# Expert layers: weight slots filled ahead in the preceding projection, and the first two blocks' rows made by one-hot products in the routing

## The chip, the cores and the metric

The kernel runs on one core of a Trainium2 chip. The metric is device time in microseconds of one execution, the median of three runs for the kernel before. Engines are named as in the profile: PE is TensorE (PEld its weight loads), DVE VectorE, ACT ScalarE, POOL GpSimd, SP the queue that issues most DMAs.

## The reference, cut to what matters

A hybrid layer (recurrent unit, sparse attention, gated linear attention, feed-forward) is followed by a second block of two layers: an SSD mixer and a dilated attention mixer, each ending in an output projection with residual and layer norm, and each followed by a mixture of experts. The sequence has 512 tokens of width 1024, all in float32. The change touches only what lies around the two expert layers:

```python
def _hierarchical_moe(x, w_rg, b_rg, w_re, b_re, w_gate, w_up, w_down):
    g_w, g_idx = lax.top_k(jax.nn.softmax(g_logits, axis=-1), 1)      # 1 of 4 groups
    e_w, e_idx = lax.top_k(jax.nn.softmax(e_logits, axis=-1), 2)      # 2 of its 8 experts
    ...
    def expert_block(args):
        xb, e = args
        h = jax.nn.silu(xb @ w_gate[e]) * (xb @ w_up[e])
        return h @ w_down[e]
```

There are 32 experts; w_gate and w_up are 1024 x 512, w_down is 512 x 1024, each 2 MB in float32. Every token goes through two experts, and their outputs are summed with the gate weights.

## The kernel before, in words

`second_block` (L3221) calls for each of the two layers a mixer (`ssd` L2202, `attention` L3043) and then `moe` (L2466). Each mixer ends in `project_model` (L484), the output projection: SP loads the weight row tiles (L505), DVE splits each into a high and a low part (L523, L525), PE multiplies (L538, L548), and the layer norm tail (`LayerNormTail`, L739) normalises token tile by token tile; its SP part (L752) loads the norm's rows and the router's weights. All products of the projection are counted on the semaphore `done`.

A kernel is a chain of stages (L62). In a stage every engine runs its own instruction list; at its end all engines meet at a barrier, and POOL clears the semaphores of an earlier stage. A DMA that is in flight is not waited for by the barrier, only by whoever waits for its semaphore.

`moe` runs two stages. In the first, `moe_route` (L2489), SP stores x to DRAM as x_rows (L2525), for the gathers, and issues nine weight loads: gate, up and down of experts 0 and 1 into slots 0 and 1 (L2529), and, after the router product, of expert 2 into the third slot (L2532), which is made of two buffers that are free there. PE computes the router logits (L2563) and turns them (L2568). DVE chooses the two experts of each token as one-hot rows `oh` (L2617 to L2635). PE ranks each token within its expert and counts the tokens of each expert (L2576, L2579; DVE waits for `counted` at L2643). DVE computes the block and the row of each token (L2646 to L2673), PE makes the lists of rows by one-hot products (L2584, after `placed`), DVE writes them as indices (L2686 to L2688). A block holds up to 64 rows of one expert; blocks 0 to 31 are the experts' first blocks, later ones the overflow. `keep_running(n)` (L2691) issues n products of the identity, whose result nobody reads: 26 and 28 in the routing and 30 at the start of the next stage.

In the second, `moe_experts` (L2704), the blocks alternate between two sets of buffers s. Per block b:

- POOL copies the block's indices to `ex_col` (L2775) and gathers its rows from x_rows (L2778). The gather of block b + 2 waits till the rows of block b are turned (L2795), and POOL issues it after the scatter of block b - 1 and before the scatter of block b.
- PE turns the rows (`turn_x`, L2812), ACT copies them to `xT` (L2877).
- PE multiplies by gate and up, one on each half of the columns of the array (`gate_up`, L2821); ACT makes silu (L2881), DVE multiplies (L2920).
- PE turns the result (`turn_h`, L2829), ACT copies it (L2885), PE multiplies by down (L2838), ACT copies the result (L2890), and POOL scatters it to y_rows (L2785, L2700).

The order on PE is written out for the first blocks (L2842 to L2859) and then looped: gate/up of block b, down of block b - 1, turn_x of block b + 1, turn_h of block b. The weights' order is SP's (L2740 to L2753): gate and up of block b go out when gate/up of the slot's last user is finished (`gate_up_ready`), down when that user's down is finished:

```python
def load(b, e, slot, users):
    for which, used in ((GATE, gate_up_ready), (UP, gate_up_ready), (DOWN, down_ready)):
        sp.wait_ge(used, users)
        sp.dma_start(raw[slot][which], ...).then_inc(w_loaded[slot][which], 16)
load(3, 3, 0, 1)
load(4, 4, 1, 2)
load(5, 5, 0, 4)
```

From block 3 on only slots 0 and 1 are used. At the end SP loads the rows of y_rows back (L2761), and DVE adds them to x with a layer norm.

## Time and profile before

| | |
|---|---|
| median of three runs | 3425.83 us (3418.22 to 3431.83) |
| the profiled execution | 3431.23 us, its span 3429.3 us |
| mean granted clock of PE | 0.923 |
| busy: PE, DVE, ACT, POOL | 3036.2, 1153.5, 852.2, 472.7 us |
| HBM read, written | 596.61 MB, 24.16 MB |
| expert weight loads | 64 of each of gate, up and down, 2048 KB each |

The profile gives the busy time of each engine; times are microseconds from the span's start, and the duration of a group in order of time is its length from first start to last end. A product in float32 makes two MATMUL records, so "x32" are 16 products. PEclk is the granted clock as a share of 2.4 GHz: 1.00 is that level, 0.50 is 1.2 GHz. A DMA share of 1.0 means that the core's 16 DMA engines were busy throughout. In brackets stands how long the engine was idle before an instruction and what released it. The expert layer after the SSD mixer is called layer 0 here (its routing begins at about 1899), the one after attention layer 1 (at about 2831).

### The profile page before, as it was taken

The numbers are of one execution on the slowest core, as the hardware profiler recorded it, in microseconds if no ns is written. First come the engines' busy times: TensorE is split into PE (matmuls) and PEld (weight loads), VectorE is DVE, ScalarE is ACT, GpSimd is POOL, SyncE is SP. The second block draws the span as 40 slices with busy tenths as digits, with TensorE's granted clock in tenths as the row PEclk, the third lists the DMA queues.
The fourth block names the chain that finished last, engine by engine and source line by source line (L and its number), as shares of the span: only waits on it lengthen the run. The fifth ranks groups of instructions, "written<-read, shape, count | busy, mean of one in ns | idle before, by whom it ended". The sixth has DMA issues, their size and how long they took to land. (4 is left out here: it accounts for less than half of the span.)

```text
span 3429.3 us, 41635 instructions
## 1 busy us (share of the span) xinstructions
PE 3036.2 (89%) x16071; PEld 2153.8 (63%) x16071; DVE 1153.5 (34%) x1825; ACT 852.2 (25%) x1731; POOL 472.7 (14%) x670
## 2 busy tenths in 40 slices
PE   7998989899989999999899887888599888888875
PEld 6787769777868878789678533333278765333332
DVE  3553754333353333437364300000253462000002
ACT  2514741332233310114450111111111341111111
POOL 0132510000000000000260111111122321111110
PEclk9998999999989999999689899988799998998897
DMA  3242022133333322222002799999733108999996
GB/s 125 86 103 75 2 74 87 39 86 86 91 93 98 98 85 92 89 84 62 2 30 83 311 362 402 406 397 400 281 114 102 36 21 349 367 394 392 403 399 254
DMA packets 250616, 605.24 MB, mean 176 GB/s; under 512 B 39829, under 2 KB 204051, under 8 KB 225788
## 3 DMA queue, kind: packets, MB, share of 16 engines
q1 hardware_dynamic: 238268, 583.05, 46.9%
q0 software_dynamic: 10880, 16.83, 1.4%
q10 hardware_dynamic: 1344, 3.67, 0.5%
q8 instruction: 82, 1.34, 0.2%
q14 instruction: 42, 0.34, 0.0%
HBM read 596.61 MB, written 24.16 MB: 181 GB/s over the span
## 5 line engine op out<-in xcount | busy, mean ns | idle before, releaser
L2821 PE MATMUL bank<-moe_raw,ex_xT 128*64 128x512 f32 x1984 | 532.7, 698 | 147.2 <-DMA moe_raw<-in_moe_w_up 144.2
L2821 PEld LDWEIGHTS bank<-moe_raw,ex_xT 128*64 128x64 f32 x1984 | 181.2, 159 | 452.4 <-issue 448.0
L2920 DVE TENSOR_TENSOR ex_h<-ex_gate,bank 64x512 f32<-64x512 f32 x64 | 44.1, 690 | 986.9 <-ACT ex_gate L2881 986.9
L248 PE MATMUL bank<-hT_hi,cut_lo 128*128 128x512 f32 x1248 | 313.0, 393 | 0.0
L248 PE MATMUL bank<-hT_hi,ahead 128*128 128x512 f32 x624 | 257.1, 412 | 28.2 <-DVEq L421 16.7
L248 PEld LDWEIGHTS bank<-hT_hi,cut_lo 128*128 128x128 f32 x1248 | 234.5, 188 | 53.3
L248 PE MATMUL bank<-hT_lo,ahead 128*128 128x512 f32 x624 | 254.8, 408 | 0.0
L248 PE MATMUL bank<-hT_hi,cut_hi 128*128 128x512 f32 x624 | 245.0, 393 | 1.2 <-DVE cut_hi L277 1.2
L248 PE MATMUL bank<-hT_lo,cut_hi 128*128 128x512 f32 x624 | 244.6, 392 | 0.0
L2838 PE MATMUL bank<-moe_raw,ex_hT 128*64 128x512 f32 x992 | 224.6, 592 | 1.3 <-ACT ex_hT L2885 1.3
L2881 ACT ACTIVATE ex_gate<-bank 64x512 f32<-64x512 f32 x64 | 37.8, 591 | 666.4 <-PE bank L2821 666.4
L2838 PEld LDWEIGHTS bank<-moe_raw,ex_hT 128*64 128x64 f32 x992 | 80.8, 137 | 132.3 <-issue 132.3
L248 PEld LDWEIGHTS bank<-hT_hi,ahead 128*128 128x128 f32 x624 | 122.8, 197 | 62.7 <-ACTq L1942 11.4
L248 PEld LDWEIGHTS bank<-hT_lo,ahead 128*128 128x128 f32 x624 | 122.7, 197 | 29.8 <-issue 0.2
L277 DVE CAST cut_hi<-raw 128x2048 fp32r<-128x2048 f32 (+1 forms) x66 | 63.8, 966 | 223.1 <-PE bank L248 136.4
L248 PEld LDWEIGHTS bank<-hT_hi,cut_hi 128*128 128x128 f32 x624 | 117.2, 188 | 28.2 <-DVE cut_hi L277 2.1
L248 PEld LDWEIGHTS bank<-hT_lo,cut_hi 128*128 128x128 f32 x624 | 117.2, 188 | 26.3 <-issue 0.2
L279 DVE TENSOR_TENSOR cut_lo<-raw,cut_hi 128x2048 fp32r<-128x2048 f32 (+1 forms) x66 | 120.4, 1824 | 2.3
L100 POOL CAST ahead<-raw 128x2048 fp32r<-128x2048 f32 x5 | 10.6, 2112 | 778.1 <-DMA raw<-in_ssd_w_in 385.0
L2785 POOL COPY moe_to<-moe_place 128x1 uint32 x64 | 11.6, 181 | 767.5 <-ACT moe_y L2890 767.5
L248 PE MATMUL bank<-cut_lo,hT_hi 128*128 128x256 f32 x768 | 108.1, 283 | 0.9 <-DVE cut_lo L279 0.3
L2812 PEld LDWEIGHTS bank<-ident,moe_x 64*128 64x128 f32 x528 | 63.2, 200 | 70.7 <-issue 70.7
(568 smaller groups left out, 5415.1 us busy)
## 6 DMA issues: line engine op xcount, KB each, us to landing
moe_raw<-in_moe_w_gate SPq DMA_DIRECT2D x62, 2048.0 KB, 14.0
moe_raw<-in_moe_w_up SPq DMA_DIRECT2D x62, 2048.0 KB, 18.5
moe_raw<-in_moe_w_down SPq DMA_DIRECT2D x62, 2048.0 KB, 9.6
raw<-in_w_in SPq DMA_DIRECT2D x26, 1024.0 KB, 5.4
raw<-in_w_ffn_in SPq DMA_DIRECT2D x44, 512.0 KB, 5.0
raw<-in_ssd_w_in SPq DMA_DIRECT2D x20, 1024.0 KB, 5.2
raw<-in_attn_w_qkv SPq DMA_DIRECT2D x18, 1024.0 KB, 5.1
raw<-in_w_in SPq DMA_DIRECT2D x24, 512.0 KB, 4.3
```

The costliest lines, as they stand in the source:

```text
L100: self.nc.gpsimd.tensor_copy(self.K.ahead[:, 0:self.words], self.K.raw[:, 0:self.words])
L248: last = nc.tensor.matmul(out, a(pa, k), b(pb, k), start=(late == "hi" and k == 0 and n == 0), stop=(late == "lo" and k == kt - 1 and n == ...
L277: nc.vector.tensor_copy(hi, raw).then_inc(rounded, 1)
L279: return nc.vector.tensor_tensor(lo, raw, hi.bitcast(F32), ALU.subtract)
L2785: nc.gpsimd.tensor_copy(to[:, s:s + 1], place[:, ds(b, 1)]).then_inc(directed, 1)
L2812: last = nc.tensor.transpose(TX[:, k * ER:(k + 1) * ER], x[:, s, k:D:KD], K.ident[0:ER, 0:ER])
L2821: last = nc.tensor.matmul(GU[s][rows, :], xT[:, s, k * ER:(k + 1) * ER], raw[slot][which][:, k * HID:(k + 1) * HID], start=(k == 0), stop= ...
L2838: last = nc.tensor.matmul(DB[s][rows, :], hT[:, s, k * ER:(k + 1) * ER], raw[slot][DOWN][:, k * D + half * HID:k * D + (half + 1) * HID], ...
L2881: nc.scalar.activation(gate[:, s, :], GU[s][left, :], ACT.Silu).then_inc(gate_done, 1)
L2920: nc.vector.tensor_tensor(h[:, s, :], gate[:, s, :], GU[s][right, :], ALU.mult).then_inc(h_ready, 1)
```

## The change

The two expert slots get fixed places in SBUF, known before the mixer runs (`ExpertSlots`), so that they can be filled while the mixer's output projection is still running. Slot 0 is loaded after the projection's own loads, gate and up of slot 1 when the projection's products are all done. In the routing, down of slot 1 and the third slot follow. In the routing the rows of blocks 0 and 1 are no longer gathered: DVE compares each token's rank among experts 0 and 1 with 0 to 63, which gives one-hot columns, and PE multiplies x, which lies in SBUF by token, by them; the result is `xT` for both blocks, already turned. Gate/up of block 0 is also made in the routing, and behind it gate and up of block 3 are loaded into slot 0. The stage of the experts starts with gate/up of block 1, and its gathers with block 2. The 28 and 30 filler products are gone. In the attention layer the projection's split weights lie at another place (`cut_at`).

```diff
@@ project_model @@
+                if slots:
+                    slots.load(sp, 0, 0, (GATE, UP, DOWN))
+                    sp.wait_ge(done, 2 * TT)
+                    slots.load(sp, 1, 1, (GATE, UP))
                 if then and begin:
@@ new @@
+FIRST = 2
+class ExpertSlots:
+    WORDS = 6 * WN
+    def __init__(self, nc, K, A, layer):
+        self.base = nc.sbuf_base
+        matrix = lambda n: self.base + 4 * n * WN
+        self.places = ((matrix(0), matrix(1), matrix(4)), (matrix(2), matrix(3), matrix(5)))
...
+    def load(self, sp, slot, e, matrices):
+        for which in matrices:
+            sp.dma_start(self.raw[slot][which], self.weights[which][e]).then_inc(self.loaded[slot][which], 16)
@@ moe_route, sync @@
-                for e in range(2):
-                    for which in range(3):
-                        sp.dma_start(raw[e][which], weights_d[which][e]).then_inc(K.w_loaded[e][which], 16)
+                K.slots.load(sp, 1, 1, (DOWN,))
                 sp.wait_ge(product_ready, 1)
-                for which in range(3):
-                    sp.dma_start(raw[2][which], weights_d[which][2]).then_inc(K.w_loaded[2][which], 16)
+                K.slots.load(sp, 2, 2, (GATE, UP, DOWN))
+                sp.wait_ge(first_gate_up, 1)
+                K.slots.load(sp, 0, 3, (GATE, UP))
@@ moe_route, tensor @@
                 last.then_inc(counted, 1)
-                keep_running(nc, K, 28)
+                pe.wait_ge(dealt, 1)
+                for k in range(KD):
+                    for t in range(TT):
+                        last = nc.tensor.matmul(first_bank[:, k], K.x[:, t, k:D:KD], first_oh[:, t], start=(t == 0), stop=(t == TT - 1))
+                last.then_inc(first_turned, 1)
                 pe.wait_ge(placed, 1)
...
                 last.then_inc(listed, 1)
+                pe.wait_ge(first_kept, 1)
+                pe.wait_ge(K.w_loaded[0][GATE], 16)
+                pe.wait_ge(K.w_loaded[0][UP], 16)
+                for k in range(KD):
+                    for which, rows in ((GATE, slice(0, ER)), (UP, slice(ER, 2 * ER))):
+                        last = nc.tensor.matmul(K.bank[0][rows, :], xT[:, 0, k * ER:(k + 1) * ER], raw[0][which][:, k * HID:(k + 1) * HID],
+                                                start=(k == 0), stop=(k == KD - 1))
+                last.then_inc(first_gate_up, 1)
@@ moe_route, scalar @@
+                act.wait_ge(first_turned, 1)
+                for e in range(FIRST):
+                    nc.scalar.activation(xT[:, e, :].rearrange("p (k r) -> p k r", k=KD), first_bank[:, :, e * ER:(e + 1) * ER], ACT.Copy).then_inc(first_kept, 1)
@@ moe_route, vector @@
+                done(nc.vector.tensor_scalar(first_rank[:, :, :], oh[:, 2, :, 0:FIRST], -2.0 * S, 2.0 * S, ALU.mult, ALU.add))
                 dve.wait_ge(counted, 1)
                 ranks = K.bank[1][:, 0:TT * NE].rearrange("p (t e) -> p t e", t=TT)
+                done(nc.vector.tensor_tensor(first_rank[:, :, :], first_rank[:, :, :], ranks[:, :, 0:FIRST], ALU.add))
+                nc.vector.tensor_tensor(first_oh[:, :, :, :], ..., ALU.is_equal).then_inc(dealt, 1)
@@ moe_experts, sync @@
-                load(3, 3, 0, 1)
+                load(3, 3, 0, 1, (DOWN,))
@@ moe_experts, gpsimd @@
-                gather(0, 0)
-                gather(1, 1)
+                for s in range(2):
+                    gather(s, FIRST + s)
+                for s in range(2):
+                    scatter(s, s)
                 n = pairs_used(pool)
-                with pool.Fori(0, n) as i:
+                with pool.Fori(1, n) as i:
@@ moe_experts, tensor @@
                 pe.sem_inc(y_kept, 2)
-                keep_running(nc, K, 30)
-                turn_x(0, 0)
-                gate_up(0, 0, 0, 16)
-                turn_x(1, 0)
+                pe.sem_inc(gate_up_ready, 1)
+                pe.sem_inc(x_turned, FIRST)
+                pe.sem_inc(x_kept, FIRST)
+                gate_up(1, 0, 1, 16)
                 turn_h(0, 0)
-                gate_up(1, 0, 1, 16)
                 down(0, 0, 0, 16)
@@ moe_experts, scalar @@
-                keep_x(0, 0)
                 make_gate(0, 0)
-                keep_x(1, 1)
@@ attention @@
-        project_model(nc, K, A.attn_w_o_2[0], HW // P, oT, tail(mem), cut_at=qk_at)
+        project_model(nc, K, A.attn_w_o_2[0], HW // P, oT, tail(mem), cut_at=K.slots.places[1][GATE], slots=K.slots)
```

## Rows read from the trace of the kernel before

**Rows 1.** DMA busy by slice of the span, from the page (40 slices of 85.7 us).

```profile
DMA  3242022133333322222002799999733108999996
```

**Rows 2.** chain of waits inside layer 1's expert loop: start, us, what.

```profile
2957.02 22.34 DMA moe_raw<-in_moe_w_up
2979.49 7.09 PE bank L2821 x32
2986.58 3.45 PE bank L2838 x16
```

**Rows 3.** busy time by stretch, layer 0: us, engines, clock, DMA share, GB/s.

```profile
1880.00:1890.00 10.00, 8.35 (x45) 6.79 (x43) 9.55 (x17) 4.92 (x10) 0.00 (x0) 1.00 0.00 0
1920.00:1930.00 10.00, 10.00 (x65) 10.00 (x64) 8.43 (x25) 0.00 (x0) 0.00 (x0) 0.69 0.99 421
2000.00:2010.00 10.00, 10.00 (x54) 4.57 (x50) 0.69 (x1) 1.40 (x3) 1.15 (x2) 1.00 0.66 240
```

**Rows 4.** SP's DMA issues around layer 0: start, us, line, transfer.

```profile
1857.01 1.29 SPq L729 DMA_DIRECT2D router_whole<-in_moe_w_router_expert  x1
1900.26 0.51 SPq L2529 DMA_DIRECT2D moe_raw<-in_moe_w_gate  x1
1909.07 0.45 SPq L2532 DMA_DIRECT2D raw<-in_moe_w_down  x1
1955.30 0.33 SPq L2744 DMA_DIRECT2D moe_raw<-in_moe_w_gate  x1
2008.76 0.33 SPq L2744 DMA_DIRECT2D moe_raw<-in_moe_w_down  x1
```

**Rows 5.** TensorE in order of time, layer 0: start, us, work, idle before.

```profile
1909.38 6.07 PE L2695 MATMUL bank<-ident 128*128 128x128 f32 x52
1919.10 1.60 PE L2579 MATMUL bank<-rt_oh,rt_ones 128*128 128x32 f32 x8
1920.52 9.23 PE L2695 MATMUL bank<-ident 128*128 128x128 f32 x56
1929.58 1.88 PE L2584 MATMUL bank<-rt_block_oh,rt_row_oh 128*128 128x48 f32 x16
1944.72 1.07 PE L2812 MATMUL bank<-ident,moe_x 64*128 64x64 f32 x8 [3.10 <-DMA moe_x<-x_rows,ex_col]
1946.48 8.78 PE L2821 MATMUL bank<-moe_raw,ex_xT 128*64 128x512 f32 x32 [0.69 <-ACT ex_xT L2877]
1957.36 7.09 PE L2821 MATMUL bank<-moe_raw,ex_xT 128*64 128x512 f32 x32
1964.28 3.60 PE L2838 MATMUL bank<-moe_raw,ex_hT 128*64 128x512 f32 x16
1982.34 1.06 PE L2812 MATMUL bank<-ident,moe_x 64*128 64x64 f32 x8 [2.23 <-DMA moe_x<-x_rows,ex_col]
```

**Rows 6.** other engines in order of time, layer 0.

```profile
1920.81 0.19 DVE L2646 COPY rt_cnt<-bank 128x32 f32<-128x32 f32 x1 [3.03 <-PE bank L2579]
1926.02 1.23 DVE L2665 TENSOR_TENSOR rt_row_oh<-rt_iota_r,rt_row 128x1024 f32<-128x1024 f32 x1
1932.91 2.29 DVE L2915 TENSOR_SCALAR x_tok<-x_tok 128x4096 f32<-128x4096 f32 x1 [0.54 <-PEq L69]
1933.74 1.50 POOL L2775 COPY ex_col<-moe_idx 64x1 uint32<-64x1 uint32 x1 [26.28 <-issue]
1945.83 0.60 ACT L2877 ACTIVATE ex_xT<-bank 128x512 f32<-128x512 f32 x1 [28.86 <-PE bank L2812]
```

**Rows 7.** layer 1 in order of time: SP's issue, then TensorE.

```profile
2889.54 0.34 SPq L2744 DMA_DIRECT2D moe_raw<-in_moe_w_gate  x1
2851.21 1.85 PE L2579 MATMUL bank<-rt_oh,rt_ones 128*128 128x32 f32 x8
2879.50 10.00 PE L2821 MATMUL bank<-moe_raw,ex_xT 128*64 128x512 f32 x32 [0.69 <-ACT ex_xT L2877]
2916.73 1.07 PE L2812 MATMUL bank<-ident,moe_x 64*128 64x64 f32 x8 [2.38 <-DMA moe_x<-x_rows,ex_col]
```

More of the change, by code:

```diff
@@ L481, with project_model @@
     on_pool = None
[L484 removed]
+def project_model(nc, K, w, kt, x, tail, fresh=None, begin=True, row_scale=None, cut_at=None, slots=None):
     SLOTS = 3
@@ L2463, in expert_weights @@
             A.moe_w_down_2[layer].rearrange("e (p k) m -> e p (k m)", p=P))
+class ExpertSlots:
[4 more added lines that the diff above has]
+        self.places = ((matrix(0), matrix(1), matrix(4)), (matrix(2), matrix(3), matrix(5)))
+        self.raw = [[nc.alloc_sbuf_tensor_at(f"slot{layer}_{s}_{which}", [P, WN], F32, offset=place) for which, place in enumerate(places)]
+                    for s, places in enumerate(self.places)]
+        self.raw.append([K.third[:, :WN], K.third[:, WN:], K.raw[:, :]])
+        self.raw = [[x[:, :] for x in slot] for slot in self.raw]
+        self.loaded = [[nc.alloc_semaphore(f"w_loaded{layer}_{s}_{which}") for which in range(3)] for s in range(3)]
+        self.weights = expert_weights(A, layer)
+    def load(self, sp, slot, e, matrices):
+        for which in matrices:
+            sp.dma_start(self.raw[slot][which], self.weights[which][e]).then_inc(self.loaded[slot][which], 16)
 def moe(nc, K, A, layer, tail):
@@ L2473, in moe @@
         idx, place = sb("idx", [ER, NB + 2], U32), sb("place", [P, NB], U32)
-        K.w_loaded = [[nc.alloc_semaphore(f"w_loaded{layer}_{s}_{which}") for which in range(3)] for s in range(3)]
         x, y, to = sb("x", [ER, 2, D]), sb("y", [P, 2, HID]), sb("to", [P, 2], U32)
+        xT = sb("xT", [P, 2, KD * ER])
         K.y_stored = [nc.alloc_semaphore(f"y_stored{layer}_{s}") for s in range(2)]
@@ L2479, in moe, with moe_route @@
         K.picked = [nc.alloc_semaphore(f"picked{layer}_{n}") for n in range(2 * TT)]
-        raw_at = -(-nc.sbuf_base // 32) * 32
-        with nc.sbuf_tensor(f"moe{layer}_raw", [P, 2, 3, WN], F32) as raw:
-            picked = nc.alloc_sbuf_tensor_at(f"picked{layer}", [P, 2, TT, D], F32, offset=raw_at)
-            K.tail_junk = nc.alloc_sbuf_tensor_at(f"tail_junk{layer}", [P, D], F32, offset=raw_at + 4 * 2 * TT * D)
-            raw = [[raw[:, s, which, :] for which in range(3)] for s in range(2)] + [[K.third[:, :WN], K.third[:, WN:], K.raw[:, :]]]
-            moe_route(nc, K, A, layer, weight, expert, pairs, idx, place, raw, x, y, to)
-            moe_experts(nc, K, A, layer, expert, pairs, idx, place, raw, x, y, to, weight, picked, tail)
-def moe_route(nc, K, A, layer, weight, expert, pairs, idx, place, raw, x, y, to):
+        picked = nc.alloc_sbuf_tensor_at(f"picked{layer}", [P, 2, TT, D], F32, offset=at)
+        K.tail_junk = nc.alloc_sbuf_tensor_at(f"tail_junk{layer}", [P, D], F32, offset=at + 4 * 2 * TT * D)
+        K.w_loaded = K.slots.loaded
+        moe_route(nc, K, A, layer, weight, expert, pairs, idx, place, K.slots.raw, x, y, to, xT)
+        moe_experts(nc, K, A, layer, expert, pairs, idx, place, K.slots.raw, x, y, to, xT, weight, picked, tail)
+def moe_route(nc, K, A, layer, weight, expert, pairs, idx, place, raw, x, y, to, xT):
     K.x_rows = nc.dram_tensor(f"x_rows{layer}", (S, D), F32, kind="Internal").ap()
-    weights_d = expert_weights(A, layer)
     with ExitStack() as mem:
@@ L2701, in store_rows, with moe_experts @@
                                  in_=y[:, s, :], in_offset=None, bounds_check=4 * S - 1, oob_is_err=False).then_inc(K.y_stored[s], 16)
-def moe_experts(nc, K, A, layer, expert, pairs, idx, place, raw, x, y, to, weight, picked, tail):
+def moe_experts(nc, K, A, layer, expert, pairs, idx, place, raw, x, y, to, xT, weight, picked, tail):
     weights_d = expert_weights(A, layer)
@@ L2739, in _, with load @@
             def _(sp):
-                def load(b, e, slot, users):
-                    for which, used in ((GATE, gate_up_ready), (UP, gate_up_ready), (DOWN, down_ready)):
+                def load(b, e, slot, users, matrices=(GATE, UP, DOWN)):
+                    for which in matrices:
+                        used = down_ready if which == DOWN else gate_up_ready
                         sp.wait_ge(used, users)
                         sp.dma_start(raw[slot][which], weights_d[which][ds(e, 1)].rearrange("e p f -> p (e f)")).then_inc(w_loaded[slot][which], 16)
-                load(3, 3, 0, 1)
+                load(3, 3, 0, 1, (DOWN,))
                 load(4, 4, 1, 2)
@@ L3225, in second_block @@
     for layer, mixer in enumerate((ssd, attention)):
-        K.router, K.tail_junk = Router(nc, K, A, layer), None
+        K.router, K.tail_junk, K.slots = Router(nc, K, A, layer), None, ExpertSlots(nc, K, A, layer)
         mixer(nc, K, A, norm(layer, 0, K.hT))
```

21 lines of the change are left out of this document (13 added, 8 removed).

## The prediction

> **What bounds the kernel now.** I began with the page's row of DMA busy time [rows 1]: of 40 slices, two runs stand at 9, and these are the two expert layers. Each streams 32 experts of three 2 MB matrices (6.3 MB), and nothing else in the kernel loads DMA so heavily. The chain of waits in such a stretch [rows 2] alternates a long DMA piece of 18 to 22 us with 7.1 us of gate/up and 3.5 us of down. The DMA piece covers the landing of one load; TensorE needs about 13 us for a block, and the chain takes some 33.6 us for two blocks. In the long middle of a layer the transfer stream is therefore the clock. An earlier start of that stream moves the end of the layer by the same amount, and a faster engine there moves nothing.
>
> Next I asked where the stream is not running. The stretches by 10 us [rows 3] show three things in layer 0: nothing moves at 1880 to 1890 while the preceding projection ends, 421 GB/s at a share of 0.99 during the routing, and a share of only 0.66 at 2000 to 2010. SP's issues [rows 4] say why. The nine loads of blocks 0 to 2 leave from 1900.26 to 1909.5 and last till about 1954. The next goes out at 1955.30, when the gate/up product of block 0 has freed slot 0. The last hole ends with the issue at 2008.76; from there DMA stays at a share near 1.0 to the layer's end. Up to that hole the order is set by TensorE [rows 5]: products to count the ranks, 28 filler products, the list at 1929.58, a barrier, 30 fillers, a wait for gathered rows till 1944.72, their transposes, the copy by ScalarE [rows 6], then gate/up of block 0 from 1946.48 to 1955.26. So the question is how much earlier gate/up of block 0 ends, and what of that is kept till the last hole.
>
> **The change part by part.**
>
> *Loads moved into the projection.* Slot 0 (6.3 MB) is issued after the router loads, at about 1858.5 [rows 4]; gate and up of slot 1 (4.2 MB) when all products of the projection are done. At 421 GB/s [rows 3] that is 15 and 10 us, and DMA is idle or nearly so there. It takes 10.5 MB or 25 us per layer out of the routing. This alone gives nothing: the stream would only stop sooner, at about 1927, and wait for slot 0. It is what permits gate/up of block 0 inside the routing. The issues cost SP about 0.4 to 1.3 us each [rows 4], with nothing urgent behind them. 25 us per layer, 50 in all, is the ceiling.
>
> *One-hot rows in the routing.* Counts are ready at 1920.7 and VectorE takes them at 1920.81 [rows 5, 6]. The small multiply-add before that wait lies in its 3 us of idle time. After it come one small addition (0.2 us, as the copy in rows 6) and a comparison of 512 elements per partition, half of the 1024 that take 1.23 us [rows 6], 0.6 us. So TensorE starts at about 1921.7. The 32 products have the shape of the fillers: 26 of those took 6.07 us, 0.233 each, with the clock at full [rows 5]; 32 are 7.5 us at the 2.4 GHz level and 15 at 1.2 GHz. In the trace the granted clock averages 0.69 over 1920 to 1930 [rows 3], so it stood at the lower level for some 6 us, and 28 fillers took 9.23 us [rows 5]. With 4.4 us of that dip left, 9 products run at half clock and 23 at full: 9.7 us, to 1931.4. Bounds 7.5 and 15; I take 9.7 because the dip is in both layers at this place.
>
> *Its operand is strided.* The stationary operand x_tok is read at every eighth float. The nearest row is the transposes of gathered rows, strided alike: eight loads in 1.07 us, 0.134 each [rows 5], against 0.117 for a contiguous filler. So the 64 loads would take 8.6 instead of 7.5 us at most; I charge nothing and keep 1.1 us for the range. The Trainium skill (SBUF — State Buffer, Door 1: The DMA port swizzle) says instead that reads which leave a 16-byte line with each element pay a penalty. By that rule these loads would be slower than contiguous ones; the row hardly shows it, but with 64 partitions, not 128. It is the slow rival below.
>
> *The list and the extra copy.* The list products wait for VectorE, now 0.9 us later (about 1929.4), and for TensorE, 1931.4; they take 1.9 us [rows 5], to 1933.3. The two copies of xT (0.60 us each, rows 6) lie beside them.
>
> *Gate/up of block 0 in the routing.* It begins at 1933.4. A gate/up takes 7.09 us at full clock [rows 5]; 8.78 and 10.0 where a dip fell into it [rows 5, 7]. I take 8.0, so it ends at 1941.4. What vanishes from before it: barrier, fillers, gather, transposes, copy (1931.5 to 1946.5). The next load goes out at 1941.5 instead of 1955.3: **13.8 us earlier**. In layer 1 the counts end at 2853.06 [rows 7]; plus 1.0, 9.7, 1.9, 8.0 and 0.1 makes 2873.8 against 2889.54: **15.7 us earlier**. It gains more because gate/up took 10.0 us there.
>
> *The barrier now lies behind gate/up.* SP issues two loads behind it (0.9 us) and TensorE resumes some 0.55 us after the last engine [rows 6]. From the end of gate/up(0) to the end of down(0) were 12.6 us [rows 5]. Now: 1.5 + 7.1 (gate/up 1) + 0.65 + 0.5 (turn and copy h) + 3.5 = 13.3 to 13.7, so **1.1 us lost** per layer. If SP or the clearing of semaphores drags, up to 3.
>
> *Gathers.* Those of blocks 2 and 3 are issued first after the barrier, at about 1943.5. From copying the index to the first transpose took 11.0 us (1933.74 to 1944.72, rows 5, 6), so block 2's rows are there at about 1955, when down(0) ends: no wait, bounds 0 and 3. Block 3's used to be queued on GpSimd behind the scatter of block 0, and TensorE waited 2.23 and 2.38 us [rows 5, 7]. That wait goes. Late next is block 4, still queued behind the scatter of block 1: 3 us of GpSimd work and 9.5 to 11 of landing against 12.8 us of TensorE work, up to 1.2 us of waiting. I keep **1.7 us gained** per layer, bounds 0 and 4.
>
> *The removed fillers* (28 and 30) never delayed a load. Their cover is the clock; see the first rival. The longer semaphore list and three VectorE instructions in the layer cost under 0.3 us.
>
> *Sum:* 13.8 − 1.1 + 1.7 = 14.4 and 15.7 − 1.1 + 1.7 = 16.3, together 30.7 us. The profiled execution took 3431.23 us (span 3429.3), so the same execution would take 3400.5. It stands 5.4 above the median 3425.83, from which the forecast is 3395.
>
> **The rivals.**
>
> *Clock lost with the fillers.* TensorE now idles about 1 us before the one-hot products where fillers ran. In the rows a dip to half follows stretches with gaps although fillers ran [rows 3, 5]. If all 32 products run at 1.2 GHz (15 us) and gate/up takes 10.0, each layer loses 5.3 + 2.0, in all 14.6, and the gain is 16: 3410. The Trainium skill (TensorE: Matmul & The Clock Gate, Part 1) states that idleness takes the array's clock to half and sustained work gives it back; by it this case could come in either layer. For it: three new short waits. Against: the routing is denser in real work than it was. Chance 0.15, about two thirds of it still beyond 0.5%.
>
> *No dip at all.* Products 7.5 and gate/up 7.1: 3.1 us more per layer, 3389. Against it: dips in both layers [rows 3, 7]. Chance 0.10.
>
> *The one-hot products are slow.* If strided 128-row loads cost 0.58 us each, 64 take 37 us instead of 9.7; each layer loses 27.3 against a gain of 14.4 to 16.3, in all +24: 3450. It decides from about 0.39 us per load, where 25 us eat the gain. Nearest row 0.134 [rows 5]: chance 0.06.
>
> *The early loads give nothing*, since the issue after the routing is not what sets the end, or the slots are not filled ahead. Then about 3426. Against it: the share of 0.66 just before 2010 [rows 3], holes that only TensorE's progress explains. Chance 0.05.
>
> **How the numbers follow.** Forecast 0.64. About 0.5% (17 us) is what a measurement can tell from no change. Faster: 0.64 + 0.10 + 0.10 = 0.84; same: 0.05 + 0.05 = 0.10; slower 0.06. The range goes from the dip-free case less the spread of runs (3418 to 3432) and the upper bound of the gather term, 3378, to the clock case with 3 us for the barrier, 3413.
>
> **What would show it.** Slot 0's loads near 1858 and slot 1's near 1887; x_tok products ending by 1932; the first load into a freed slot near 1941 and 2874; DMA idle some 14 us between 1927 and 1941; steady two-block periods of 33.6 us unchanged; the last hole ending 14 us earlier. Wrong: products of x_tok over 15 us, a gather wait over 3 us at block 2, or a layer whose stream starts earlier but ends at the same distance from its start.

## The result and the profile after

The changed kernel takes 3407.31 us in the median of 20 runs (3396.29 to 3418.59), the kernel before 3429.86 us in 20 runs on the same chips (3417.73 to 3443.50). The ratio is 0.9938, 95% interval 0.9925 to 0.9951: 22.5 us less, where I had forecast 30.7 less (3395 us). The profiled execution took 3402.02 us with a span of 3400.0; its mean granted clock is 0.925 (before 0.923).

DMA busy by slice of the span, after, to be held against [rows 1]. Ahead of the first run of nines 2 and 7 have become 4 and 6, ahead of the second 0 and 8 have become 2 and 6: bytes have moved to earlier slices.

```profile
DMA  3242022134333322222004699999833126999996
```

Busy time by stretch of layer 0, after (columns as in [rows 3]):

```profile
1880.00:1890.00 10.00, 9.12 (x48) 7.42 (x46) 9.56 (x20) 4.40 (x9) 0.00 (x0) 1.00 0.18 44
1890.00:1900.00 10.00, 3.14 (x17) 2.54 (x18) 8.73 (x12) 3.58 (x6) 0.00 (x0) 0.64 0.88 375
1920.00:1930.00 10.00, 8.95 (x40) 8.82 (x40) 7.65 (x24) 0.00 (x0) 0.00 (x0) 0.66 0.74 316
1930.00:1940.00 10.00, 10.00 (x52) 9.85 (x54) 2.40 (x10) 1.08 (x2) 0.00 (x0) 1.00 0.01 2
1940.00:1950.00 10.00, 7.82 (x38) 2.56 (x36) 2.47 (x4) 1.88 (x2) 0.78 (x1) 1.00 0.25 74
2000.00:2010.00 10.00, 9.84 (x46) 4.03 (x48) 0.69 (x1) 0.79 (x2) 2.21 (x3) 1.00 0.97 386
```

The same two stretches in the kernel before:

```profile
1930.00:1940.00 10.00, 8.41 (x61) 8.32 (x61) 3.75 (x9) 0.00 (x0) 3.67 (x4) 0.83 1.00 424
1940.00:1950.00 10.00, 6.21 (x33) 3.56 (x33) 0.00 (x0) 1.88 (x2) 1.14 (x2) 0.84 1.01 372
```

The early loads run: 375 GB/s at 1890 to 1900. Then the stream has nothing left to fetch, from about 1927 to 1947: shares 0.01 and 0.25 where it was 1.00 and 1.01 before. That is 20 us of idle DMA where I had reckoned with 14. At 2000 to 2010 the share is 0.97 instead of 0.66, so the last hole has moved forward. SP's issues say by how much (after, layer 0; to be held against [rows 4]):

```profile
1859.08 3.01 SPq L2491 DMA_DIRECT2D slot<-in_moe_w_gate  x1
1887.40 0.33 SPq L2491 DMA_DIRECT2D slot<-in_moe_w_gate  x1
1900.56 0.42 SPq L2554 DMA_DIRECT2D x_rows<-x_tok  x1
1946.83 0.33 SPq L2491 DMA_DIRECT2D slot<-in_moe_w_gate  x1
1960.85 0.33 SPq L2792 DMA_DIRECT2D slot<-in_moe_w_down  x1
1998.29 0.33 SPq L2792 DMA_DIRECT2D slot<-in_moe_w_down  x1
```

Gate of block 3 leaves at 1946.83 (before 1955.30), down of block 3 at 1960.85, and down of block 5, which ends the last hole, at 1998.29 (before 2008.76). The routing starts 0.76 us later in this execution, so from here on I count from the issue of the x_rows store (1900.56 after, 1899.80 before). What TensorE does in that time, after, layer 0 (to be held against [rows 5]):

```profile
1922.57 15.48 PE L2613 MATMUL bank<-rt_first_oh,x_tok 128*128 128x128 f32 x64 [1.05 <-DVE rt_first_oh L2691]
1937.89 1.88 PE L2617 MATMUL bank<-rt_block_oh,rt_row_oh 128*128 128x48 f32 x16
1939.70 7.09 PE L2625 MATMUL bank<-slot,moe_xT 128*64 128x512 f32 x32
1948.97 7.09 PE L2871 MATMUL bank<-slot,moe_xT 128*64 128x512 f32 x32 [2.18 <-PEq L2895]
1957.15 3.65 PE L2888 MATMUL bank<-slot,ex_hT 128*64 128x512 f32 x16 [0.47 <-ACT ex_hT L2934]
1960.98 1.06 PE L2862 MATMUL bank<-ident,moe_x 64*128 64x64 f32 x8 [0.18 <-DMA moe_x<-x_rows,ex_col]
```

and in layer 1 ([rows 7] before):

```profile
2841.23 15.48 PE L2613 MATMUL bank<-rt_first_oh,x_tok 128*128 128x128 f32 x64 [1.05 <-DVE rt_first_oh L2691]
2858.36 7.09 PE L2625 MATMUL bank<-slot,moe_xT 128*64 128x512 f32 x32
2867.97 8.78 PE L2871 MATMUL bank<-slot,moe_xT 128*64 128x512 f32 x32 [2.52 <-PEq L2895]
```

The one-hot products take 15.48 us, in both layers, against my 9.7. The list is as I wrote, gate/up of block 0 is 0.9 us shorter, the barrier behind it cost 1.4 and 3.4 us against my 1.1, and the wait for block 2's rows is 0.18 us. The middle of the layer is as it was: the chain has pieces of DMA of some 18 to 22 us, and between them 7.1 to 10 us of gate/up and 3.5 us of down on TensorE, as before ([rows 2] shows one such round).

### The profile page after: what moved, and what is told of

Its sections match the earlier page's. It is cut to its first block and busy times, and to the rows that moved or that the text cites. A ratio compares the mean times of both kernels' runs of the same rounds, so it can differ in the third digit from the quotient of the medians.

```text
span 3400.0 us, 41341 instructions
## 1 busy us (share of the span) xinstructions
PE 3023.7 (89%) x15935; PEld 2146.2 (63%) x15935; DVE 1154.3 (34%) x1831; ACT 852.0 (25%) x1731; POOL 469.5 (14%) x662
## 5 line engine op out<-in xcount | busy, mean ns | idle before, releaser
L2871 PE MATMUL bank<-slot,moe_xT 128*64 128x512 f32 x1920 | 512.2, 694 | 146.6 <-DMA slot<-in_moe_w_up 139.9
L2871 PEld LDWEIGHTS bank<-slot,moe_xT 128*64 128x64 f32 x1920 | 176.6, 159 | 439.2 <-issue 432.1
L2888 PE MATMUL bank<-slot,ex_hT 128*64 128x512 f32 x992 | 224.8, 592 | 2.3 <-ACT ex_hT L2934 2.3
L2888 PEld LDWEIGHTS bank<-slot,ex_hT 128*64 128x64 f32 x992 | 80.8, 137 | 132.3 <-issue 131.0
L248 PEld LDWEIGHTS bank<-hT_hi,ahead 128*128 128x128 f32 x624 | 123.7, 198 | 62.3 <-ACTq L1946 11.4
L277 DVE CAST cut_hi<-raw 128x2048 fp32r<-128x2048 f32 (+1 forms) x66 | 63.8, 967 | 222.8 <-PE bank L248 136.1
L100 POOL CAST ahead<-raw 128x2048 fp32r<-128x2048 f32 x5 | 10.5, 2092 | 777.6 <-DMA raw<-in_ssd_w_in 385.2
L2833 POOL COPY moe_to<-moe_place 128x1 uint32 (+1 forms) x64 | 11.7, 183 | 730.3 <-ACT moe_y L2939 730.3
L248 PE MATMUL bank<-ahead,hT_hi 128*128 128x256 f32 x384 | 95.6, 284 | 6.3 <-DVEq L421 6.3
```

The source lines that it names most:

```text
L100: self.nc.gpsimd.tensor_copy(self.K.ahead[:, 0:self.words], self.K.raw[:, 0:self.words])
L248: last = nc.tensor.matmul(out, a(pa, k), b(pb, k), start=(late == "hi" and k == 0 and n == 0), stop=(late == "lo" and k == kt - 1 and n == ...
L277: nc.vector.tensor_copy(hi, raw).then_inc(rounded, 1)
L2833: nc.gpsimd.tensor_copy(to[:, s:s + 1], place[:, ds(b, 1)]).then_inc(directed, 1)
L2871: last = nc.tensor.matmul(GU[s][rows, :], xT[:, s, k * ER:(k + 1) * ER], raw[slot][which][:, k * HID:(k + 1) * HID], start=(k == 0), stop= ...
L2888: last = nc.tensor.matmul(DB[s][rows, :], hT[:, s, k * ER:(k + 1) * ER], raw[slot][DOWN][:, k * D + half * HID:k * D + (half + 1) * HID], ...
```

## The experiments

All are compared with the kernel before on the same chips. Since single executions of one kernel lie up to 23 us from its median, I read two things of each: the median, and the distance of the last hole's end (the issue of block 5's down load) from the x_rows store in its profiled execution. A hole is a stretch in which the stream of weight loads stands still. "Holes" is the sum over both layers less the 220.0 us of before; "time" is the difference of the medians.

| kernel | block 3's down (layers 0, 1) | block 5's down | holes | time | ratio, 95% interval |
|---|---|---|---|---|---|
| before | 68.1, 70.0 | 109.0, 111.0 | 0 | 0 | 1 |
| the change | 60.3, 62.3 | 97.7, 99.3 | -22.9 | -22.5 | 0.9938 [0.9925, 0.9951] |
| the change again | 60.2, 62.2 | 98.1, 99.5 | -22.4 | -20.7 | 0.9938 [0.9921, 0.9956] |
| early loads alone | 63.3, 63.0 | 104.9, 105.0 | -10.1 | -7.4 | 0.9976 [0.9957, 0.9994] |
| the same, no 30 fillers | 63.3, 63.8 | 104.1, 105.4 | -10.5 | -6.6 | 0.9975 [0.9964, 0.9987] |
| one-hot rows alone | 60.2, 62.1 | 100.5, 99.2 | -20.3 | -14.6 | 0.9957 [0.9939, 0.9975] |
| contiguous slices of x | 55.9, 56.0 | 93.2, 95.2 | -31.6 | | a single execution, 3400.6 us |
| x copied ahead | 55.9, 56.1 | 93.5, 93.0 | -33.4 | -29.0 | 0.9915 [0.9887, 0.9943] |
| x copied ahead, again | 55.9, 56.1 | 93.4, 93.1 | -33.4 | -28.3 | 0.9910 [0.9896, 0.9925] |
| and earlier gathers | 54.3, 54.9 | 94.0, 91.8 | -34.2 | -38.0 | 0.9888 [0.9867, 0.9908] |
| and earlier gathers, again | 54.0, 54.0 | 93.9, 93.2 | -32.8 | -30.2 | 0.9896 [0.9873, 0.9919] |
| gate/up of block 0 late | 62.2, 62.7 | 99.6, 101.9 | -18.5 | -17.5 | 0.9951 [0.9935, 0.9967] |
| products made twice | 77.1, 77.3 | 116.3, 114.2 | +10.5 | +13.3 | 1.0030 [1.0009, 1.0050] |

The last hole puts kernels whose holes differ by more than 2 us in the order of their times (closer neighbours change places, as -20.3 and -18.5 do), and misses the time by 6 us at most. The end of the last hole is a good place to read this change, also where my numbers for it were not. What differs between the kernels ahead of the store does not explain them: from the load of the router's expert weights to the x_rows store are 42.8 us in layer 0 and 35.0 to 35.1 in layer 1, in the kernel before, in the changed one and in those with either half alone, so the early loads do not lengthen the projection.

### The early loads alone

The kernel before with `ExpertSlots` and the loads of slot 0 and of gate and up of slot 1 in the projection; rows gathered, fillers kept, gate/up of block 0 in the experts' stage.

```diff
@@ kernel before: project_model and moe_route, sync @@
+                if slots:
+                    slots.load(sp, 0, 0, (GATE, UP, DOWN))
+                    sp.wait_ge(done, 2 * TT)
+                    slots.load(sp, 1, 1, (GATE, UP))
...
-                for e in range(2):
-                    for which in range(3):
-                        sp.dma_start(raw[e][which], ...)
+                K.slots.load(sp, 1, 1, (DOWN,))
```

> The kernel before with the early loads alone: slot 0 and gate/up of slot 1 filled in the projection, rows gathered and gate/up of block 0 made as before. Theory (TensorE's chain up to the last hole in the stream sets the layer's end): block 3's gate/up load still goes out some 55 us after the store of x_rows in each layer, DMA only stands idle some 25 us longer before it, and the time is that of before, 3430 within 5 us. Rival (bytes taken out of the routing shorten the layer): up to 25 us a layer, 3380 to 3405.

Measured 3422.04 us (12 runs) against 3429.4: 7.4 us less. That is small, but the interval ends at 0.9994, just short of 1. The prediction said "this alone gives nothing", and that fell. Its trace, layer 0 (GpSimd and TensorE in order of time, x_rows stored at 1897.83):

```profile
1934.21 1.00 POOL L2801 DMA_INDIRECT moe_x<-x_rows,ex_col  x1 [0.93 <-POOL ex_col L2798]
1939.59 1.09 PE L2835 MATMUL bank<-ident,moe_x 64*128 64x64 f32 x8
1941.37 7.09 PE L2844 MATMUL bank<-slot,ex_xT 128*64 128x512 f32 x32 [0.69 <-ACT ex_xT L2900]
```

The rows are there 5.4 us after their gather's issue or sooner, and TensorE goes from the fillers to the transposes without a wait. In the kernel before the same gather was issued at 1936.16 and the transposes began at 1944.72 [rows 5], 8.6 us later, after a wait of 3.10. From the gather's issue to the transposes DMA's share was 1.00 there and is 0.21 here. And since TensorE did not idle, gate/up takes 7.09 instead of 8.78 us, and 7.09 instead of 10.0 in layer 1. In layer 0 the two parts, 3.2 us at the transposes and 1.7 at gate/up, are the 4.8 us by which block 3's gate leaves earlier (+50.67 instead of +55.50). So the idle stream was worth something after all: the gather of 64 rows no longer runs beside 2 MB loads.

### The same without the fillers

```diff
@@ moe_experts, tensor @@
                 pe.sem_inc(y_kept, 2)
-                keep_running(nc, K, 30)
                 turn_x(0, 0)
```

> The kernel before with the early loads alone and without the 30 filler products at the head of the experts' stage. With the fillers its rows of block 0 were turned at 1939.59, with no wait, 5.4 us after their gather was issued. Theory A: with DMA idle at that moment the rows land within 3 to 5 us of the issue, so the fillers had become what TensorE waits for; without them turn_x starts 1 to 2 us earlier, and the layer keeps it if gate/up still takes 7.1 us: ratio to the kernel before 0.996 to 0.997 instead of 0.9976. Theory B: the idle time before the rows takes the granted clock to half again, the first gate/up takes 8.8 to 10 us, and the gain is lost: 0.998 or more. If instead the rows land 8 us after the issue, as in the kernel before, my reading that an idle DMA is what makes the early loads worth 7 us is wrong.

Measured 3421.4 us (12 runs), ratio 0.9975, as with the fillers. The mechanisms of both theories are there, and they cancel (layer 0, x_rows stored at 1886.80):

```profile
1923.13 1.00 POOL L2801 DMA_INDIRECT moe_x<-x_rows,ex_col  x1 [0.92 <-POOL ex_col L2798]
1926.21 1.12 PE L2835 MATMUL bank<-ident,moe_x 64*128 64x64 f32 x8 [8.08 <-DMA moe_x<-x_rows,ex_col]
1928.01 9.42 PE L2844 MATMUL bank<-slot,ex_xT 128*64 128x512 f32 x32 [0.69 <-ACT ex_xT L2899]
```

```profile
1920.00:1925.00 5.00, 0.00 (x0) 0.00 (x0) 2.17 (x1) 0.00 (x0) 2.71 (x3) 0.50 0.03 6
1925.00:1930.00 5.00, 3.11 (x14) 1.72 (x16) 0.00 (x0) 1.88 (x2) 2.12 (x3) 0.50 0.21 60
```

The rows are used 3.1 us after the issue (1923.13), with DMA at a share of 0.12 between the two: the transposes start 39.4 us after the store instead of 41.8. But TensorE idled 8 us ahead of them, the granted clock stands at 0.50, and gate/up takes 9.42 us instead of 7.09. Block 3's gate leaves at +50.67 with the fillers and without them; in layer 1 it leaves at +51.2 instead of +50.4. In layer 0 the 2.4 us gained are paid back to the hundredth, in layer 1 with 0.9 us more, and taking the fillers out alone buys nothing.

### The one-hot rows alone

The changed kernel with all six loads of slots 0 and 1 back in the routing.

```diff
@@ changed kernel: project_model and moe_route, sync @@
-                if slots:
-                    slots.load(sp, 0, 0, (GATE, UP, DOWN))
-                    sp.wait_ge(done, 2 * TT)
-                    slots.load(sp, 1, 1, (GATE, UP))
...
-                K.slots.load(sp, 1, 1, (DOWN,))
+                for e in range(2):
+                    K.slots.load(sp, e, e, (GATE, UP, DOWN))
```

> The changed kernel without the early loads: all of slots 0 and 1 are issued at the start of the routing, one-hot rows and gate/up of block 0 in the routing stay. Theory: TensorE's chain is as early as in the changed kernel, so block 3's gate/up goes out about 46 us after the store of x_rows (55.5 before); the stream then has almost no hole left, and the holes of before summed to 10 or 11 us a layer, so the gain against before is 16 to 21 us: 3409 to 3414. Rival (the early loads are what the gain needs): 3425 to 3430.

Measured 3414.83 us (12 runs): 14.6 us less than before, just short of the 16 to 21 that I expected. SP and TensorE in layer 0 (x_rows stored at 1898.78), and the stretches:

```profile
1920.78 15.48 PE L2610 MATMUL bank<-rt_first_oh,x_tok 128*128 128x128 f32 x64 [1.05 <-DVE rt_first_oh L2688]
1937.91 7.09 PE L2622 MATMUL bank<-slot,moe_xT 128*64 128x512 f32 x32
```

```profile
1945.04 0.33 SPq L2487 DMA_DIRECT2D slot<-in_moe_w_gate  x1
```

```profile
1930.00:1940.00 10.00, 10.00 (x53) 8.63 (x54) 1.32 (x8) 1.08 (x2) 0.00 (x0) 1.00 0.99 421
1940.00:1950.00 10.00, 7.91 (x38) 2.69 (x36) 2.98 (x2) 1.88 (x2) 1.65 (x2) 1.00 1.00 426
```

Block 3's gate leaves at +46.26, to 0.01 us where it leaves with the early loads. Gate/up of block 0 in the routing doesn't need them: slot 0, issued first there, is in before the products are done. The stream runs through to 1950. With the early loads some 20 us of idle DMA stand in its place (summed from the shares of stretches of 5 us from 1925 to 1950), and the last hole ends 2.8 us sooner in layer 0 and 0.1 later in layer 1. The early loads move 25 us of transfer per layer out of the routing and some 20 us of it come back as a hole. As times the two halves (-7.4 and -14.6) sum to -22.0 against -22.5 for the whole, but their holes (-10.1 and -20.3) do not sum to its -22.9: the gather that the early loads speed up is gone once the rows are one-hot, so nothing shown here makes the sum of the times more than chance. The intervals of this kernel and of the whole overlap, so what the early loads add on top of the one-hot rows is some 3 us by the holes and 8 by the medians, and no better known.

### Whether the products' cost is the clock or the stride

The changed kernel, with x read as 128 adjacent columns instead of every eighth. This leaves out the interleaving of x's columns, so the rows of blocks 0 and 1 come out in another order of columns.

```diff
-                        last = nc.tensor.matmul(first_bank[:, k], K.x[:, t, k:D:KD], first_oh[:, t], ...)
+                        last = nc.tensor.matmul(first_bank[:, k], K.x[:, t, k * P:(k + 1) * P], first_oh[:, t], ...)
```

> The changed kernel with contiguous slices of x as the stationary operand; it leaves out the interleaving of the columns, so the rows of blocks 0 and 1 come out in another column order. Theory (the stride of 32 bytes slows the weight loads to 0.24 us each at either clock): a load takes 0.117 us at full clock and 0.234 at half, the 64 of them 9 to 10.5 us instead of 15.5, and gate/up of block 0 ends 5 to 6 us earlier in each layer. Rival (the clock, or the operand's 128 partitions, or the one-hot operand): they stay near 15.5 us.

Weight loads and products of that line, both layers (min/median/max in ns), in the changed kernel:

```profile
L2613 PEld LDWEIGHTS bank<-rt_first_oh,x_tok x128: 312/335/338, 1922.6 to 2856.2; 128*128 128x128 f32 x128
L2613 PE MATMUL bank<-rt_first_oh,x_tok x128: 340/402/606, 1922.6 to 2856.3; 128*128 128x128 f32 x128
```

and with adjacent columns:

```profile
L2613 PEld LDWEIGHTS bank<-rt_first_oh,x_tok x128: 192/192/333, 1922.6 to 2850.8; 128*128 128x128 f32 x128
L2613 PE MATMUL bank<-rt_first_oh,x_tok x128: 274/275/582, 1922.6 to 2850.9; 128*128 128x128 f32 x128
```

```profile
1922.65 9.51 PE L2613 MATMUL bank<-rt_first_oh,x_tok 128*128 128x128 f32 x64 [1.05 <-DVE rt_first_oh L2691]
```

9.51 us for the 64 records (8.78 in layer 1): my 9.7, clock dip and all. So the clock term was right, and the stride is the whole error of this term. The same line's records in two stretches of 3 us, one at each level of the clock, show how (columns: PE busy, PEld busy, clock, DMA share, GB/s). The changed kernel:

```profile
1923.00:1926.00 3.00, 3.00 (x14) 3.00 (x14) 0.50 0.98 421
1932.00:1935.00 3.00, 3.00 (x14) 3.00 (x14) 1.00 0.00 0
```

and with adjacent columns:

```profile
1923.00:1926.00 3.00, 3.00 (x15) 3.00 (x15) 0.50 1.02 437
1928.00:1931.00 3.00, 3.00 (x30) 3.00 (x29) 1.00 0.01 5
```

Adjacent loads double their rate with the clock; strided ones keep it, 14 in 3 us at 1.2 as at 2.4 GHz, and with DMA idle as with DMA at 421 GB/s (the counts include the records that the edges of a stretch cut). Since the edit changes nothing but the step, what limits them is neither the clock nor traffic on DMA but the strided operand, 15.48 / 64 = 0.242 us per 128 x 128 load. At half clock that costs almost nothing over adjacent columns; at full clock it halves the rate.

### x copied ahead

To keep the interleaving and still load adjacent columns, ScalarE and VectorE copy x into that order at the start of the routing, where both are idle, into the buffer of the third slot's down, whose load then waits for the products.

```diff
@@ scalar (and vector, for the other two tiles) @@
+                for t in range(TT // 2):
+                    nc.scalar.activation(x_even[:, t], in_columns(t), ACT.Copy).then_inc(spread_act, 1)
@@ tensor @@
-                        last = nc.tensor.matmul(first_bank[:, k], K.x[:, t, k:D:KD], first_oh[:, t], ...)
+                        last = nc.tensor.matmul(first_bank[:, k], x_even[:, t, k], first_oh[:, t], ...)
@@ sync @@
-                K.slots.load(sp, 2, 2, (GATE, UP, DOWN))
+                K.slots.load(sp, 2, 2, (GATE, UP))
+                sp.wait_ge(first_turned, 1)
+                K.slots.load(sp, 2, 2, (DOWN,))
```

> The changed kernel with x first copied to the order that the products want, two tiles by ScalarE and two by VectorE at the start of the routing, where both wait 8 to 10 us for the router product; down of the third slot, whose buffer holds the copy, is loaded after the products. Theory: each copy takes 1 to 2 us in idle time, the products 9 to 10.5 us instead of 15.5, gate/up of block 0 ends 5 us earlier a layer, and the last hole closes as much earlier: 3395 to 3400. Rival: strided copies take longer than the idle time or the stream becomes the bound again, and it stays at 3405 to 3410.

> The version with x copied ahead once more, as the base of the next on the same chip. 0.9915 to the kernel before by the first comparison, between 0.989 and 0.994.

Measured 3400.4 us (6 runs, ratio 0.9915) and 3399.7 us (6 runs on another chip, ratio 0.9910): 29.0 and 28.3 us less than before, near what the prediction forecast for the change itself (30.7). It was not timed beside the changed kernel on one chip: against 0.9938 [0.9925, 0.9951] the first interval overlaps and the second only touches. The copies and the products in layer 0:

```profile
1900.08 4.15 ACT L2638 ACTIVATE raw<-x_tok 128x1024 f32<-128x1024 f32 x2 [1.56 <-PEq L69]
1900.10 2.12 DVE L2664 COPY raw<-x_tok 128x1024 f32<-128x1024 f32 x2 [0.32 <-PEq L69]
1922.83 9.47 PE L2619 MATMUL bank<-rt_first_oh,raw 128*128 128x128 f32 x64 [1.14 <-DVE rt_first_oh L2701]
1943.12 8.78 PE L2881 MATMUL bank<-slot,moe_xT 128*64 128x512 f32 x32 [2.09 <-PEq L2905]
```

They end 18 us before they are needed. The products take 6.0 us less (6.7 in layer 1), but in layer 0 the clock now dips in the gate/up of block 1, 8.78 instead of 7.09 us (in layer 1 it did so in the changed kernel too), and the last hole ends 4.2 and 6.3 us sooner.

### The products made twice

```diff
-                for k in range(KD):
+                for k in [*range(KD), *range(KD)]:
                     for t in range(TT):
```

> The changed kernel with the 32 one-hot products made twice over (the second pass overwrites the first with the same values); nothing else differs. Theory A: from the end of the ranks to the last hole in the stream TensorE's chain sets the time, microsecond for microsecond. The second pass adds 15.5 us to the chain in each layer: gate and up of block 3 are issued +61.8 us after the x_rows store instead of +46.3, the last hole ends 15.5 us later in each layer (near +113 and +115 instead of +97.7 and +99.3), and the time is 31 us above that of the changed kernel, 3438 us or 8 us above the kernel before (ratio about 1.003). Theory B: some of the chain is slack (the list of rows, the gathers or the loads of slot 1 and the third slot end it instead), so less than 10 us of the 15.5 arrive at the last hole, and the time stays under that of the kernel before (ratio 0.999 or less).

> The changed kernel once more, on the same chip as the three others of this batch, as their base. By the first comparison its ratio to the kernel before is 0.9938; between 0.9925 and 0.9951 if nothing depends on the chip. Its one-hot products take 15.5 us again, and block 3's gate and up leave at +46.3.

Measured 3443.97 us (12 runs) against 3409.96 for the change again: 34.0 us more for 2 x 15.24 us of products, and slower than the kernel before (ratio 1.0030). Theory A's number was 31 and 1.003. TensorE and SP in layer 0 (x_rows stored at 1900.06):

```profile
1922.04 30.72 PE L2613 MATMUL bank<-rt_first_oh,x_tok 128*128 128x128 f32 x128 [1.05 <-DVE rt_first_oh L2691]
1963.62 8.78 PE L2871 MATMUL bank<-slot,moe_xT 128*64 128x512 f32 x32 [2.12 <-PEq L2895]
```

```profile
1961.54 0.33 SPq L2491 DMA_DIRECT2D slot<-in_moe_w_gate  x1
```

Block 3's gate leaves at +61.5, 15.2 later, and the holes end 32.9 us later in both layers together; part of what exceeds the 30.5 is gate/up of block 1 in layer 0, 8.78 us instead of 7.09. There is no slack on this chain, which is why the price of the products decided the result.

### Gate/up of block 0 put back

The changed kernel with gate/up of block 0, and the loads that follow it, at the head of the experts' stage.

```diff
@@ moe_route, sync and tensor @@
-                sp.wait_ge(first_gate_up, 1)
-                K.slots.load(sp, 0, 3, (GATE, UP))
...
-                last.then_inc(first_gate_up, 1)
@@ moe_experts, sync and tensor @@
-                load(3, 3, 0, 1, (DOWN,))
+                load(3, 3, 0, 1)
-                pe.sem_inc(gate_up_ready, 1)
+                gate_up(0, 0, 0, 16)
                 gate_up(1, 0, 1, 16)
```

> The changed kernel with gate/up of block 0 put back to the head of the experts' stage, its weights long loaded; gate and up of block 3 are then issued in that stage too. The early loads and the one-hot rows stay. Theory A: the work that TensorE does up to down of block 0 is the same, and the barrier of some 2.3 us lies in front of it instead of in its middle; the issue of block 3's gate and up comes 2 to 3 us later (about +49 instead of +46.3), but the down of block 0 ends at the same distance (about +60.3 and +62.3), the last hole ends within 1.5 us of the changed kernel's, and the time is the same within 3 us (ratio to the kernel before 0.993 to 0.995). Theory B: each microsecond by which block 3's load leaves later is lost for good, as my forecast reckoned for that issue: the last hole ends 2.5 us later in each layer, and the time is 5 us above the changed kernel's (ratio 0.9953).

Measured 3413.22 us (6 runs), 3.3 us above the change again; the intervals overlap. In the trace block 3's gate leaves 4.4 and 4.8 us later (+50.6, +51.0); block 3's down 2.0 and 0.5 later; the last hole ends 1.5 and 2.4 us later.

```profile
1931.74 15.65 PE L2861 MATMUL bank<-slot,moe_xT 128*64 128x512 f32 x64 [2.04 <-PEq L2884]
```

The issue moves by more than I expected because the clock dips here too: gate/up of blocks 0 and 1 take 15.65 us together (16.28 in layer 1), against 7.09 each in the changed kernel's layer 0. The truth lies between the theories: not each microsecond of that issue is lost, since the stream catches up in the next hole, but a third to a half is. By the holes that part of the change is worth 3.9 us, by the medians 3.3, which the intervals do not tell from nothing.

### Earlier gathers and four fillers

The version with x copied; GpSimd gathers block b + 2 before it scatters block b - 1, and four fillers stand behind gate/up of block 0.

```diff
@@ gpsimd @@
-                for s in range(2):
-                    scatter(s, s)
+                scatter(0, 0)
...
                         gather(s, i * 2 + s + 2)
-                        scatter(s, i * 2 + s)
+                        scatter(1 - s, i * 2 + s - 1)
+                scatter(1, n * 2 - 1)
@@ moe_route, tensor @@
                 last.then_inc(first_gate_up, 1)
+                keep_running(nc, K, 4)
```

> The version with x copied into contiguous order ahead of the one-hot products, with two additions. GpSimd issues the gather of block b + 2 before the scatter of block b - 1 instead of after it, from block 4 on; and four filler products stand behind gate/up of block 0 in the routing, beside SP's two issues. Theory A: the waits for gathered rows at blocks 4 and 5 (0.7 and 1.6 us) vanish, gate/up of block 1 takes 7.1 us instead of 8.8 because TensorE idles for 1.2 instead of 2.1 us before it, so the last hole ends 2 to 4 us earlier in each layer than without the additions (+90 to +91 instead of +93.5 and +93.0), and the time is 4 to 7 us less: 3394 us, ratio 0.990. Theory B: those waits lie beside transfers that end later anyway, the last hole stays within 1 us of +93, and the time of the two versions is the same within 2 us (ratio 0.9915).

> The version with x copied, the earlier gathers and four fillers once more. The first comparison gave 0.9888 against 0.9915 of the version without the two additions, with intervals that overlap, while the last hole of its trace lay only 0.7 us per layer earlier. Theory A (the additions save time on the way to the last hole): the ratio of the two versions on one chip is 0.998 or less. Theory B (they do nothing that reaches the end, as the last holes say): within 0.1% of each other.

Measured 3392.69 us and, again beside the version without the additions, 3397.82 against 3399.70 us (ratios 0.9896 and 0.9910, with intervals that overlap). The first time was near theory A's, the second comparison, 0.06% apart, is theory B's. The trace of the first, layer 0:

```profile
1940.42 1.16 PE L2754 MATMUL bank<-ident 128*128 128x128 f32 x8
1942.63 7.09 PE L2882 MATMUL bank<-slot,moe_xT 128*64 128x512 f32 x32 [1.05 <-PEq L2906]
1955.55 1.07 PE L2873 MATMUL bank<-ident,moe_x 64*128 64x64 f32 x8 [1.09 <-DMA moe_x<-x_rows,ex_col]
1957.31 8.78 PE L2882 MATMUL bank<-third,moe_xT 128*64 128x512 f32 x32 [0.21 <-ACT moe_xT L2937]
```

The four fillers did their part: 1.05 us idle instead of 2.09, and gate/up of block 1 takes 7.09 us. But TensorE then comes to block 2's rows before they are there, waits 1.09 us, and the dip falls into the next gate/up, 8.78. Of 1.7 us gained nothing is left in layer 0. (The two additions were not run apart.) The last hole stays at +94.0 and +93.9 there. In layer 1 it ended 1.2 us sooner once and 0.1 later once. Over both comparisons this version was the fastest that I ran, but whether it beats the one without the additions stays open.

## Why the prediction was off

The direction, the place and the method held; the sum was 30.7 us where 22.5 were measured, and 22.9 at the last holes. By its own terms:

- **One-hot products, 9.7 us: this term failed.** They took 15.48 us, 5.8 more per layer, 11.6 in all. "I charge nothing" for the strided operand was the wrong choice between row and rule. The row that I took as nearest, transposes of gathered rows at 0.134 us per load [rows 5], has the same step but 64 partitions, not 128, and transposes instead of multiplying; the loads here took 0.242 us. Which of the two differences makes it cheap no run separates. The Trainium skill (SBUF — State Buffer, Door 1: The DMA port swizzle) says that reads whose elements leave a 16-byte line pay; every eighth float is a step of 32 bytes. The trace agrees for these loads, and the measured price is 15.5 against 9.5 us; for the transposes, weight loads of 202 ns at the median against 192 for adjacent ones, it shows hardly any. The slow rival had the right mechanism at the wrong size: 0.242, not 0.58, a price for which I had named no row, and below its point of decision, 0.39. I had given it a chance of 0.06 as a whole and nothing for a price in between, which is what came; it lies even beyond my upper bound of 15 us.
- **The clock.** 4.4 us of dip was about right (9.51 and 8.78 us with adjacent columns), but the strided loads hid it, since they run at one rate at either level. Gate/up of block 0 took 7.09 us in both layers, not 8.0: 0.9 gained each. The rival of all products at half clock would have given nearly the same 15 us for another reason; the stretch at clock 1.00 with 14 records in 3 us excludes it.
- **Block 3's load.** Forecast 13.8 and 15.7 us earlier, measured 9.2 and 11.2 (+55.5 to +46.3, +57.4 to +46.2). Of the 4.6 and 4.5 us missing per layer the two terms above account for all (5.8 - 0.9 = 4.9).
- **The barrier behind gate/up.** Forecast 1.1 us lost; block 3's down came 7.8 us earlier in both layers, so 1.4 and 3.4 were lost. In layer 1 the idle time of 2.52 us before gate/up of block 1 brought a dip (8.78 us). That clock cost I had placed only before the barrier.
- **Gathers.** Forecast 1.7 us gained, bounds 0 and 4. From block 3's down to block 5's were 40.8 and 41.0 us before, and 37.4 and 37.0 after: 3.4 and 4.0 gained. The term was too small because it held only the wait at block 3 (2.23 and 2.38 us) and not the clock behind it. Gate/up of block 3 took 8.78 us before, in both layers, and takes 7.09 now (layer 0, before and after):

```profile
1984.09 8.78 PE L2821 MATMUL bank<-moe_raw,ex_xT 128*64 128x512 f32 x32 [0.20 <-ACT ex_xT L2877]
1974.97 7.09 PE L2871 MATMUL bank<-slot,moe_xT 128*64 128x512 f32 x32 [0.21 <-ACT moe_xT L2926]
```

Wait and dip were 3.9 and 4.1 us. Less the waits that are there now (in layer 0 0.18 us at block 2 and 0.31 at block 4, in layer 1 none) that is 3.4 and 4.1, against 3.4 and 4.0 measured.
- **"This alone gives nothing", "it is what permits gate/up of block 0 inside the routing".** Both wrong. Alone the early loads gave 7.4 us, through a gather that is there sooner on an idle DMA and a clock that does not dip behind it; and gate/up stands at the same place without them. In the sum it did little harm, since the gather they speed up is the one that the one-hot rows remove.

Sum of the misses, over both layers: -11.6 + 1.8 - 2.6 + 4.0 = -8.4, against 7.8 at the last holes (30.7 - 22.9) and 8.2 in the medians (30.7 - 22.5). The range, 3378 to 3413, held the result because its upper end had been stretched for a slower clock, which did not come; a slower operand did. That part was luck. The test "products of x_tok over 15 us" had been written down as a sign that the forecast is wrong, and with 15.48 us it came true.

## What to carry to other kernels

Time given back in one queue counts only as far as the next thing it waits for lets it: find the last hole in the bounding stream, and price every instruction between the change and that hole: here each microsecond added to TensorE in the routing arrived at the end, while of a mere reordering behind it a third to a half did. When a product reads its stationary operand with a step, price it from rows of the same instruction, partitions and step at full clock, and if ScalarE or VectorE idle ahead of it, let them lay it out first: two tiles each, 2 to 4 us in idle time, were worth 6 us of TensorE per layer. What an engine gains by starting sooner and what it loses because the fillers that held its clock are gone can cancel within a microsecond; look at the next product's duration before counting the gain.

## What I had not expected of the hardware

- A 128 x 128 float32 weight load with a step of 32 bytes keeps one rate, 0.242 us over the 64 records, at 1.2 and at 2.4 GHz and with DMA idle or at 421 GB/s; with adjacent columns the rate doubles from the one level to the other (15 and 30 records in 3 us).
- A gather of 64 rows was usable 8.6 us after its issue with DMA at a share of 1.00 in between, at most 5.4 at 0.21, and 3.1 at 0.12 (layer 0 of three kernels).
- After idle times of 2.1 to 2.5 us gate/up ran partly at half clock in some places and not in others: layer 0 of the changed kernel kept 7.09 us after 2.18, with x copied it took 8.78 after 2.09 in layer 0 and after 2.19 in layer 1. Which of them dips I could not tell from the length of the idle time.
- The pace of the transfer stream differs between executions, 16.2 to 16.6 us per block over the last 24 of a layer; layer 0 of the changed kernel had 16.22 once and 16.48 once. Over the 26 blocks behind the last hole the two ends lie 10 us apart in each layer, an estimate from these paces, which is enough for the scatter of single times, and the reason to read distances in the trace and medians.
